# The last expert's rows added by TensorE from SBUF instead of through DRAM, in a token mixer and mixture-of-experts layer

## What is computed

```python
h = layer_norm(ALPHA * x + hybrid_token_mixer(x, ...), ln1_g, ln1_b)     # h is h1 below, ALPHA = 2 ** 0.25
# hierarchical_moe(h): the best of 4 groups, then the best 2 of its 8 experts, for each token
combine = sum(one_hot(global_idx, 32) * weights[..., None], axis=1)
hg = einsum("td,edf->tef", h, exp_w_gate)
hu = einsum("td,edf->tef", h, exp_w_up)
hid = silu(hg) * hu * combine[:, :, None]
ffn = einsum("tef,efd->td", hid, exp_w_down)
out = layer_norm(ALPHA * h + ffn, ln2_g, ln2_b)
```

## Time and profile before

| what | value |
|---|---|
| median of 3 runs (lowest, highest) | 460.43 us (458.83, 460.63) |
| the profiled execution: its time | 457.27 us |
| its span, first to last instruction | 455.5 us |
| PE busy | 415.1 us, 91% of the span |
| DVE, ACT, POOL busy | 187.6, 107.5, 84.9 us |
| mean granted clock of PE, 1 = 2.4 GHz | 0.98 |
| DMA | 139.09 MB, 305 GB/s in the mean |

### The profile page before, as it was taken

The page is one execution under the profiler, slowest core; times in us unless marked ns, Lnnn a source line. Parts: engine busy times, 40 slices in busy tenths (PEclk is TensorE's granted clock), DMA queues, the critical chain, the costliest instruction groups (busy, mean ns, idle before and its releaser), DMA issues.

```text
span 455.5 us, 6659 instructions
## 1 busy us (share of the span) xinstructions
PE 415.1 (91%) x2588; PEld 281.8 (62%) x2588; DVE 187.6 (41%) x372; ACT 107.5 (24%) x175; POOL 84.9 (19%) x116
## 2 busy tenths in 40 slices
PE   7999999999999999889999999997967988868882
PEld 6888766888888888655555655555544645444330
DVE  2579222999745485763212222212112112120085
ACT  3442457751140014101111111111101111111311
POOL 2500000000000003162233332233113101011033
PEclk9999999999999999999999999999989989999997
DMA  8956222022379999399999999999999999998383
GB/s 293 276 192 202 94 92 90 4 94 92 109 279 391 413 416 383 138 370 358 408 407 408 411 406 408 413 409 411 411 411 410 409 415 413 415 416 331 142 337 139
DMA packets 44479, 139.09 MB, mean 305 GB/s; under 512 B 5287, under 2 KB 15559, under 8 KB 40358
## 3 DMA queue, kind: packets, MB, share of 16 engines
q1 hardware_dynamic: 38288, 126.89, 71.8%
q0 software_dynamic: 6144, 11.84, 7.3%
q10 hardware_dynamic: 22, 0.02, 0.0%
HBM read 134.41 MB, written 12.58 MB: 323 GB/s over the span
## 4 chain that ended last, share of the span: by engine, by line
PE 71%; DMA 19%; SPq 3%; DVE 3%; issue 1%; ACT 1%; DVEq 0%; POOLq 0%
PE bank L1047 18%; DMA wgu<-in_exp_w_up 16%; PE bank L878 11%; PE bank L879 11%; PE bank L880 11%; PE bank L1066 8%; PE bank L1125 2%; PE bank L1037 2%; PE bank L1057 2%; PE bank L930 2%; SPq L494 2%; DMA raw<-in_w_in 1%; DMA pair_y<-y_pairs 1%; SPq L491 1%; PE bank L977 1%
## 5 line engine op out<-in xcount | busy, mean ns | idle before, releaser
L1047 PE MATMUL bank<-wgu,xTg 128*64 128x256 f32 x992 | 120.3, 397 | 19.9 <-DMA wgu<-in_exp_w_up 18.8
L1047 PEld LDWEIGHTS bank<-wgu,xTg 128*64 128x64 f32 x992 | 74.9, 143 | 56.4 <-issue 17.9
L1425 DVE TENSOR_TENSOR hid<-gated,bank 64x256 f32<-64x256 f32 x32 | 13.5, 422 | 125.6 <-ACT gated L811 125.6
L878 PE MATMUL bank<-xT_hi,w_hi 128*128 128x512 f32 x160 | 62.8, 393 | 1.8 <-DVE w_lo L1158 1.8
L652 POOL DMA_INDIRECT y_pairs<-ys,y_rows x32 | 32.3, 1011 | 161.0 <-PE bank L1037 106.0
L879 PE MATMUL bank<-xT_lo,w_hi 128*128 128x512 f32 x160 | 62.3, 390 | 0.0
L880 PE MATMUL bank<-xT_hi,w_lo 128*128 128x512 f32 x160 | 62.3, 389 | 0.0
L1066 PE MATMUL bank<-wdn,hidT 128*64 128x512 f32 x248 | 58.7, 593 | 0.9 <-issue 0.9
L811 ACT ACTIVATE gated<-bank 64x256 f32<-64x256 f32 x32 | 12.1, 379 | 158.6 <-PE bank L1047 158.6
L1144 DVE TENSOR_TENSOR w_lo<-raw,w_hi 128x2048 fp32r<-128x2048 f32 x12 | 27.5, 2291 | 33.0 <-ACT w_hi L726 32.9
L726 ACT ACTIVATE w_hi<-raw 128x2048 fp32r<-128x2048 f32 x12 | 23.0, 1920 | 59.9 <-PE bank L880 53.2
(11 more groups left out here) (237 smaller groups left out, 429.3 us busy)
## 6 DMA issues: line engine op xcount, KB each, us to landing
wgu<-in_exp_w_gate SPq DMA_DIRECT2D x31, 1024.0 KB, 15.3
wgu<-in_exp_w_up SPq DMA_DIRECT2D x31, 1024.0 KB, 21.5
wdn<-in_exp_w_down SPq DMA_DIRECT2D x31, 1024.0 KB, 20.6
raw<-in_w_in SPq DMA_DIRECT2D x9, 1024.0 KB, 5.3
raw<-in_w_out SPq DMA_DIRECT2D x4, 1024.0 KB, 5.0
pair_y<-y_pairs SPq DMA_DIRECT2D x8, 512.0 KB, 7.4
xres<-in_x SPq DMA_DIRECT2D x2, 1024.0 KB, 6.8
h_rows<-xres POOLq DMA_DIRECT2D x4, 512.0 KB, 8.0
```

The lines of the kernel that those rows point to most:

```text
L878: pe.matmul(dst, a_hi, b_hi, start=start, stop=False)
L1047: mm = pe.matmul(psum[2 + b][BLOCK * which:BLOCK * which + BLOCK, 0:F], xTg[b][:, j, h * BLOCK:(h + 1) * BLOCK], wgu[s][:, which, k, :], s ...
```

## The change

1. The last expert's `ys` is not scattered. DVE makes for each tile of tokens a matrix `last_hot` (token by slot, the token's weight where the slot is its own, else 0; twice side by side) in item 3 (`place_last`); PE turns the four in item 4, ACT copies them to `last_slots` (slot by token), and PE's item 5 waits for that copy. At the end PE multiplies `last_slots` by the `ys` in SBUF and adds to the bank; each half of the columns is a product over 64 rows of the array, rows 0 to 63 for one and 64 to 127 for the other.
2. Since nothing is written now to the `y_pairs` rows of tokens whose pair is of the last expert, all of `y_pairs` is zeroed: POOL clears a tile `zero_rows`, and SP writes it to DRAM in four parts behind the weight chunks 3 to 6. The first scatter, and the tile's later users, wait for this.
3. SP's reads of the pairs wait for 31 experts' scatters instead of 32.
4. ALPHA * h1 is no longer an f32 product with a diagonal matrix. ACT rounds ALPHA * h1 to float32r (`base_hi`), DVE makes the rest (`base_lo`), and PE adds both by products with a rounded identity (`begin_z`), for tile 0 ahead of the count of overflow items, for the others between the tiles.
5. The eight weight diagonals are made in item 29 (`make_diag`). Tile 2's second pair too is left to DVE, and the banks are numbered otherwise (`z_bank`).

The diff, without the allocations and semaphores that only name things (line numbers in `@@` are of before and after):

```diff
@@ -93,19 +93,22 @@
+        before_items = place[0]
...
+        last_slots = at("last_slots", [P, TT, P], F32, before_items)
...
@@ -238,7 +247,10 @@
-        diag = at("diag", [P, 1 + TOP_K * TT, P], F32, ring + 3 * SLOT + 8192)
+        diag = at("diag", [P, TOP_K * TT, P], F32, ring + 3 * SLOT + 8192)
+        zero_rows = at("zero_rows", [P, D], F32, shared_y)
+        base_hi = at("base_hi", [P, TT, D], F32R, ring + 4 * SLOT)
+        base_lo = at("base_lo", [P, TT, D], F32R, ring + 5 * SLOT)
...
@@ -259,13 +271,18 @@
         over_cmp = at("over_cmp", [1, MAX_OVER, N_EXP], F32, spare + 2048 * (RING + 1))
+        last_hot = at("last_hot", [P, TT, 2, BLOCK], F32, spare + 2048 * (RING + 1))
         assert place[0] >= route + 7680
-        DVE_ADDED = 1
+        DVE_ADDED = (0, 2)
         def z_of(t, h):
-            return pair_y[t][1][:, h * H:(h + 1) * H] if t < DVE_ADDED else psum[2 * t + h][:, :]
+            return pair_y[t][1][:, h * H:(h + 1) * H] if t in DVE_ADDED else z_bank(t, h)[:, :]
+
+        def z_bank(t, h):
+
+            return psum[4 * (t % 2) + 2 * h + (1 if t < 2 else 0)]
...
@@ -454,6 +479,10 @@
+        def scattered(b):
+
+            return 16 * len(range(b, N_EXP - 1, RING))
+
         def gathered(q, r):
...
@@ -485,6 +514,11 @@
                               w_in_chunk(c) if c < N_IN else w_out_chunk(c)).then_inc(raw_in[c % 2], 16)
+                if 3 <= c < 7:
+                    if c == 3:
+                        sp_.wait_ge(zero_ready, 1)
+                    part = y_pairs.rearrange("(p a) h -> p (a h)", p=P)[:, (c - 3) * 2 * D:(c - 2) * 2 * D]
+                    sp_.dma_start(part.rearrange("p (a d) -> p a d", a=2), zero_rows[:, :].unsqueeze(1).to_broadcast([P, 2, D])).then_inc(pairs_zero, 16)
...
@@ -560,10 +594,9 @@
             n = sp_.value_load(n_over[0:1, 0:1], min_val=0, max_val=MAX_OVER)
-            sp_.wait_ge(y_scattered[0], 16 * n + mains(0))
-            for i in range(N_EXP - RING, N_EXP):
-                if i % RING:
-                    sp_.wait_ge(y_scattered[i % RING], mains(i % RING))
+            sp_.wait_ge(y_scattered[0], 16 * n + scattered(0))
+            for b in range(1, RING):
+                sp_.wait_ge(y_scattered[b], scattered(b))
             for t in range(TT):
...
@@ -611,6 +644,7 @@
                 pool.memset(rg_pad[j][:, 0:PAD], 0.0).then_inc(pads_zero, 1)
+            pool.memset(zero_rows[:, :], 0.0).then_inc(zero_ready, 1)
             pool.wait_ge(raw_first[1], 16)
...
@@ -658,7 +692,7 @@
             SCATTER_LAG = 2
-            for i in range(N_EXP + SCATTER_LAG):
+            for i in range(N_EXP - 1 + SCATTER_LAG):
                 if i + RING < N_EXP:
...
@@ -666,6 +700,7 @@
                     pool.wait_ge(rows_ready, 2)
+                    pool.wait_ge(pairs_zero, 16 * 4)
                 if done >= 0:
...
@@ -739,12 +774,15 @@
             def y_split_hi(k, src):
+                if k == 0:
+                    act.wait_ge(pairs_zero, 16 * 4)
                 act.wait_ge(y_ready, k + 1)
...
             split_hi(1)
+            act.activation(ident_r[:, :], ident[:, :], ACT.Copy).then_inc(ident_rounded, 1)
             act.wait_ge(par_ready, 1)
...
@@ -820,27 +858,41 @@
+            def make_diag():
+
+                act.wait_ge(weights_ready, 1)
+                for t in range(TT):
+                    for k in range(TOP_K):
+                        act.activation(diag[:, TOP_K * t + k, :], ident[:, :], ACT.Copy, scale=weight[:, k, t:t + 1]).then_inc(diag_ready, 1)
+
+            def split_base_hi(t):
+
+                act.activation(base_hi[:, t, :], h1[:, t, :], ACT.Copy, scale=ALPHA).then_inc(base_hi_ready, 1)
+
             def act_item(q, r):
...
                 gate(q + r * RING, q % 2, 2)
+                if q == 4:
+                    act.wait_ge(last_turned, 1)
+                    act.activation(last_slots[:, :, :], psum[3][:, :].rearrange("p (t n) -> p t n", t=TT), ACT.Copy).then_inc(last_slots_ready, 1)
                 if 1 <= q < N_EXP - 1:
                     copy_main_y(q - 1, r)
+                if q == N_EXP - 3:
+                    make_diag()
             rounds(act, act_item)
+            act.wait_ge(h1_in, 16)
+            for t in range(TT - 1):
+                split_base_hi(t)
             copy_main_y(N_EXP - 1, 0)
+            split_base_hi(TT - 1)
...
             overflow(act, act_over)
-
-            act.activation(diag[:, 0, :], ident[:, :], ACT.Copy, scale=ALPHA).then_inc(diag_ready, 1)
-            act.wait_ge(weights_ready, 1)
-            for t in range(TT):
-                for k in range(TOP_K):
-                    act.activation(diag[:, 1 + TOP_K * t + k, :], ident[:, :], ACT.Copy, scale=weight[:, k, t:t + 1]).then_inc(diag_ready, 1)
...
@@ -1079,6 +1131,8 @@
                     main_down(q - 1, r)
+                if q == 5:
+                    pe.wait_ge(last_slots_ready, 1)
                 gate_up(q + r * RING, slot_of(q), q % 2, 2, loads_of(q, r))
...
@@ -1088,6 +1142,12 @@
                     sum_rows(3, MAX_OVER, over_slot, over_y_hot).then_inc(over_summed, 1)
+                if q == 4:
+
+                    pe.wait_ge(last_hot_ready, TT)
+                    for t in range(TT):
+                        mm = pe.transpose(psum[3][:, t * P:(t + 1) * P], last_hot[:, t, :, :].rearrange("p a m -> p (a m)"), ident[:, :])
+                    mm.then_inc(last_turned, 1)
                 if 1 <= q < N_EXP - 1:
...
@@ -1096,6 +1156,18 @@
             main_down(N_EXP - 1, 0)
+
+            def begin_z(t):
+
+                pe.wait_ge(base_hi_ready, t + 1)
+                pe.wait_ge(base_lo_ready, t + 1)
+                for h in range(2):
+                    cols = slice(h * H, (h + 1) * H)
+                    pe.matmul(z_bank(t, h)[:, :], ident_r[:, :], base_hi[:, t, cols], start=True, stop=False)
+                    pe.matmul(z_bank(t, h)[:, :], ident_r[:, :], base_lo[:, t, cols], start=False, stop=False)
+
+            pe.wait_ge(ident_rounded, 1)
+            begin_z(0)
...
@@ -1111,18 +1183,18 @@
             pe.wait_ge(y_copied, n + N_EXP)
-            pe.wait_ge(h1_in, 16)
-            pe.wait_ge(diag_ready, 1)
+            pe.wait_ge(diag_ready, TOP_K * TT)
             for t in range(TT):
+                last = 0 if t in DVE_ADDED else TOP_K - 1
+                if t > 0:
+                    begin_z(t)
                 for h in range(2):
-                    pe.matmul(psum[2 * t + h][:, :], diag[:, 0, :], h1[:, t, h * H:(h + 1) * H], start=True, stop=False)
-            pe.wait_ge(diag_ready, 1 + TOP_K * TT)
-            for t in range(TT):
-                last = 0 if t < DVE_ADDED else TOP_K - 1
+                    half = slice(h * BLOCK, (h + 1) * BLOCK)
+                    pe.matmul(z_bank(t, h)[:, :], last_slots[half, t, :], ys[(N_EXP - 1) % RING][half, :], start=False, stop=False)
                 for k in range(last + 1):
...
                     for h in range(2):
-                        mm = pe.matmul(psum[2 * t + h][:, :], diag[:, 1 + TOP_K * t + k, :], pair_y[t][k][:, h * H:(h + 1) * H],
+                        mm = pe.matmul(z_bank(t, h)[:, :], diag[:, TOP_K * t + k, :], pair_y[t][k][:, h * H:(h + 1) * H],
                                        start=False, stop=k == last)
...
@@ -1383,6 +1455,7 @@
             before_last()
+            v.tensor_copy(last_chosen[:, :], pairs(chosen[:, :, :, :])[:, :, N_EXP - 1])
             link(v.tensor_tensor_scan(extra_sum[:, :], extra[:, :], zeros[:, :], 0.0, ALU.add, ALU.add))
...
@@ -1418,6 +1491,20 @@
                 v.tensor_tensor(weight[:, 1, :], weight[:, 0, :], vexp[:, :], ALU.mult).then_inc(weights_ready, 1)
+                v.wait_ge(weights_ready, 1)
+
+            def place_last():
+
+                step(v.tensor_tensor(last_ranks[:, :], last_chosen[:, :], rank[:, :], ALU.mult))
+                step(v.tensor_tensor(last_weights[:, :], last_chosen[:, :], weight[:, :, :].rearrange("p k t -> p (k t)"), ALU.mult))
+                before_last()
+                step(v.tensor_tensor(last_rank[:, :], last_ranks[:, 0:TT], last_ranks[:, TT:], ALU.add))
+                before_last()
+                step(v.tensor_tensor(last_weight[:, :], last_weights[:, 0:TT], last_weights[:, TT:], ALU.add))
+                v.wait_ge(dve, chain[0])
+                for t in range(TT):
+                    v.tensor_scalar(last_hot[:, t, :, :], up_slot.unsqueeze(1).to_broadcast([P, 2, BLOCK]),
+                                    last_rank[:, t:t + 1], last_weight[:, t:t + 1], ALU.is_equal, ALU.mult).then_inc(last_hot_ready, 1)
...
@@ -1439,10 +1526,15 @@
                     take_weights()
+                    place_last()
                 make_hid(i, q % 2, 2)
...
             rounds(v, dve_item)
+            for t in range(TT):
+                v.wait_ge(base_hi_ready, t + 1)
+                v.scalar_tensor_tensor(out=base_lo[:, t, :], in0=h1[:, t, :], scalar=ALPHA, in1=base_hi[:, t, :],
```

(5 more changed lines are left out.)

21 lines of the change are left out of this document (18 added, 3 removed).

## The result

The changed kernel took 461.17 us as a median of 20 runs (459.41 to 463.20), the kernel before 459.97 beside it (457.60 to 462.92); the ratio, an estimate over all runs of both, is 1.0044 with a 95% interval of 1.0027 to 1.0062 (the two medians alone are 1.2 us apart). Two more sets, on two chips, gave 1.0045 (1.0020 to 1.0070) and 1.0042 (1.0019 to 1.0066), with medians 2.0 and 2.1 us apart. It is slower, by 0.44% or 2.0 us: less than the 0.5% that the prediction's chances are divided by, but more than no change, which was the forecast. The time lies in the range.

What follows compares the result with a forecast made beforehand. The expert weight stream and the tail after it set the end. 429.0 + 10.6 + 2.8 + 3.6 + 0.8 put PE's end at 446.8 (before 446.84); with the 8.7 tail unchanged, the median stays 460.4 us, range 457.2 to 463.8.

Steps and rivals of the forecast that it cites:

- forecast A: Tail: h1's wait and PE's added work eat the gain; 460.4 us, 458.5 to 462 within bounds; chance 0.47.
- h1's landing: Tail: h1's load lands at 425.2 us, queued behind the weights, and ACT waits for it before copying the last ys.
- PE right behind the copy: Tail: PE's first slot product starts when ACT's copy of the last ys ends, at 429.0 us.
- PE's work from there: Tail, PE from 429.0: pairs 10.6, rounded products 2.8, slot products 3.6, mode changes 0.8, ending at 446.8 us.
- rival C: Tail: the slot products' halves don't overlap on PE, costing 3.4 us, so 463.8; chance 0.15.
- rival B: Tail: PE's clock falls to half speed for 3.4 us after idling, costing 1.3 us, so 461.7; chance 0.13.
- The end: After PE's last product: the tail of DVE's normalisation, last store and close stays 8.7 us.
- The early parts: Ahead of the tail: zeroing, making the last expert's matrix, and moving the scales were costed at nothing.
- Rival D: Tail: the chain shortens by 4.6 us because reads begin sooner and h1 is not in it, so 455.8; chance 0.17.
- Rival E: Ahead of the tail: one of the early covers fails, by 3 us or more, so 463.4; chance 0.08.

Runs made afterwards that it cites:

- fill with h1 by tiles: Changed kernel with h1 loaded and rounded by tiles, count loads ahead of tile 0's h1 products, and unused products filling PE's idle: 0.9965 of the kernel before.
- one part: Changed kernel without base_lo, its eight PE products and DVE's four subtractions: 1.0009 of the kernel before.
- late reads: Changed kernel with SP's reads of the pairs held until all of h1 is rounded: 1.0139 of the kernel before.
- fill: Changed kernel plus four unused 128x512 f32 products on PE between the last down product and tile 0's h1 products: 1.0016 of the kernel before.
- slots first: Changed kernel with ACT copying the last ys before waiting for h1 and PE doing all eight slot products before h1 work: 0.9985 of the kernel before.
- h1 by tiles: Changed kernel with h1 loaded as four transfers, one per tile, and ACT's roundings waiting tile by tile: 1.0043 of the kernel before.
- all early parts: Kernel before plus early zeroing and the unused weighted matrix (place_last, four transposes, ACT's copy), tail as before: 0.9998 of the kernel before.

## Why the prediction was wrong

**The mechanism was right.** The last scatter and the pairs leave the chain, `h1` takes their place, and PE's added products eat what is left. The forecast A named this, and the fill with h1 by tiles, the one part and the late reads bear out its pieces. What was wrong is that these add up to no change. Against the terms, in us behind D (424.3 in the prediction):

- *h1's landing.* Forecast 0.9 behind D; 1.3 in both later profiles of the change, and -0.4 in the first. Three roundings 2.95 (forecast 3.2), as sized.
- *PE right behind the copy.* This step failed. I let the slot products start when the copy ends, 4.7 behind D. They start at 5.8 (the later profiles and the fill), although the copy does end 4.7 behind D there. What comes later is the other branch, which I had taken as hidden. With DVE's first `base_lo` PE can start tile 0's h1 products at 3.8 (forecast 3.3, and `h1` lands 0.4 later), they take 1.2 with the fill, and then come PE's loads of the count, in which PE issues nothing, 0.85 in the first profile, 0.83 with the fill. From `h1`'s landing to the first slot product that makes 4.5 to 4.6 in the profiles of the change, where I had 3.8. The loads' share is read from the profiles: the run that moved them moved the products too. I costed twelve products and no scalar step between them.
- *PE's work from there.* Forecast 17.8; 18.2 with the clock up. Pair products are 0.86 apart in place of 0.88, rounded ones 0.23, and the two slot products of a tile take 1.06. Had the halves run one after another, two would take 1.76: they overlap, and rival C is refuted. The Trainium skill ("TensorEngine Tiling (Array Packing)", Key Properties) warned of a drain at each change of tiling mode. The runs agree, and price it: in the slots first, four such pairs in a row take 0.91 each (427.51 to 431.14), so going back costs 0.15 of the 1.06, and going over costs 0.09 (0.32 in place of 0.23). Eight changes make 1.0, where my sum had 0.8, so that the rule is no reason for the loss.
- *The clock.* This step failed too, and it decides. I gave rival B 0.13, on the ground that real products run until D and that idles of 1.4 in the tail of before had no fall. But I had an idle of 3.3 in my own sum, and the one fall that I had looked at stood behind an idle of 2.24: that row was the nearer one, and I weighed it less. The trace of before has three more falls, each as PE starts again behind an idle of 2.3 to 3.7 (316.4, 334.9 and 352.1), and none behind its idles up to 1.9. PE idled 2.10 to 3.77. The price was sized right at 1.3: it is 0.8 to 1.7 where the later profiles of the change (PE's last product at 24.8 and 25.6) stand beside the fill's (23.9).
- *The end.* Forecast 8.7 behind PE's last product as before; 7.7 in every profile of the change, so 1.0 is gained there. DVE's chain takes the same 3.3 from PE's last product to its last half (446.84 to 450.14 before, 451.71 to 455.03 after); the rest is the last stores. They close 3.7 behind the last issue in place of 4.7, and in all twenty profiles this goes with how long before tile 3's first store tile 2's was issued: 0.9 to 1.1 in before and four others (4.7 to 4.8), 1.5 with one part (4.2), 1.9 to 2.1 in the change and the rest (3.6 to 3.8). So the last stores may wait behind tile 2's, but no run was made to test it.
- *The early parts.* Costed at nothing, measured at 0.9989 and 0.9998.

Together: +1.1 for the start, +0.4 for PE's work, +0.8 to 1.7 for the clock, -1.0 at the end: 1.3 to 2.2 slower, where 2.0 was measured. In my forecast the four stood at 0. Rival D's case, the chain shorter by 4.6, needed an h1 that isn't waited for; with that and the clock kept, h1 by tiles and fill gained 1.6 us, near the 2.0 that the prediction gave it by PE's own work. Rival E is refuted by two runs, but for `make_diag` and `ident_r`.

What stays open: why the clock falls for 3.4 in one execution and 6.8 in another of the same kernel, how much of the late start is the loads of the count, and why the last stores close 1 us sooner.

## What to carry to other kernels

A sum in which a wait falls away must also ask what the engine does meanwhile: here a PE that waits 2 to 4 us in the tail loses its clock for the work behind it, and filling the wait, with waste if need be and with real work if the order allows it, is worth something by itself (0.3% here). A remedy that seems to do nothing alone (h1 by tiles) may only have uncovered the next idle; try it with the other one before the theory is dropped. Where an in-order engine has work with few inputs (the slot products) and work with a late one (h1), the first belongs in front, and then one looks again at how the work is divided among engines, since the bound has moved.

## What the runs showed of the hardware

TensorE's granted clock fell to its lower level (0.50, so 1.2 GHz) soon after D in each of the eight profiles in which PE had idled 2.1 to 3.8 us there, and in none of the twelve (before's among them) in which its idles there were 0.4 to 1.5. Only the fills change the idle alone, the rest is what the profiles have in common. Ahead of the tail it is less tidy. Four times the same 32 products, from before, all early parts, the change's first profile and before:

```profile
334.94 5.25 PE L1047 MATMUL bank<-wgu,xTg 128*64 128x256 f32 x32 [3.65 <-DMA wgu<-in_exp_w_up]
...
325.86 3.67 PE L1078 MATMUL bank<-wgu,xTg 128*64 128x256 f32 x32 [3.53 <-DMA wgu<-in_exp_w_up]
...
410.73 5.36 PE L1099 MATMUL bank<-wgu,xTg 128*64 128x256 f32 x32 [1.81 <-DMA wgu<-in_exp_w_up]
...
408.84 3.67 PE L1047 MATMUL bank<-wgu,xTg 128*64 128x256 f32 x32 [1.58 <-DMA wgu<-in_exp_w_up]
```

The 3.67 is at full clock, the 5.25 and 5.36 are for the most part at half. An idle of 3.53 had no fall behind it, and one of 1.81 had one, so the length of the idle alone does not decide. In the tail the stretches last 3.4, 6.8 or 10.2 us. The idle that counts need not be the one that was looked at: when the first was removed, the next (2.21 for the first pair) brought the same fall.

A product of 64 rows by 512 columns in f32 on one half of the array runs beside one on the other half although both read all columns: two in 0.91 where four such pairs stand in a row, and in 1.06 where products of the whole array follow. A whole one takes 0.86.
